# A two-layer hybrid decoder trunk on one core: weights of the third expert block loaded earlier, full blocks first, experts chosen tile by tile, part of the causal mask moved

## The reference

```python
a = rmsnorm(h, mix_norm_g[i]); z = a @ w_in[i]        # split for three mixers
y_a = sgu_mixer(...)                                   # gated unit, mixes tokens in chunks of 128
y_b = conv_mixer(...)                                  # causal convolution, 31 taps, 256 channels
y_c = mla_mixer(...)                                   # 8 heads, causal attention, q and k of 96, v of 64
h = h + concat(rmsnorm(y_a), rmsnorm(y_b), rmsnorm(y_c)) @ w_o[i]
m = rmsnorm(h, ffn_norm_g[i])
h = h + hier_moe(m, ...)                               # 32 experts in 4 groups, 2 experts per token
gate = sigmoid(rmsnorm(h) @ ple_gate_w[i])
h = h + gate * rmsnorm(p[i] @ ple_proj_w[i])           # per-layer embeddings p, "projected"
```

## Time and profile before

| what | value |
|---|---|
| median of 3 runs | 2188.45 us (2186.95 to 2190.23) |
| the profiled execution | 2190.58 us, span 2188.80 us |
| TensorE busy | 2000.5 us, 91% of the span |
| VectorE busy | 1009.4 us, 46% |
| ScalarE busy | 638.8 us, 29% |
| transfers | 361.98 MB, mean 165 GB/s |

### The profile page before, as it was taken

One profiled execution on the slowest core, in us unless ns is written; L12 is line 12 of the kernel. 1 busy time (PEld: TensorE's weight loads), 2 busy tenths in 40 slices (PEclk: granted clock), 3 DMA queues, 4 the chain that ended last, 5 costly groups with the idle time before them and its releaser, 6 DMA issues.

```text
span 2188.8 us, 34749 instructions
## 1 busy us (share of the span) xinstructions
PE 2000.5 (91%) x9032; PEld 1110.8 (51%) x9032; DVE 1009.4 (46%) x2247; ACT 638.8 (29%) x1521; POOL 374.5 (17%) x542
## 2 busy tenths in 40 slices
PE   6999799899969999989979998998999699999898
PEld 3555466655535455544435554666555354445344
DVE  2489756654341111124434897566543421111253
ACT  3333355522111111131133333555221111111221
POOL 2232100021012222210022221000210122221100
PEclk9999899999979999999989998999999799999999
DMA  7011241000389999955210112410004799999422
GB/s 249 15 29 29 59 153 30 25 20 29 140 308 396 380 382 378 389 217 192 88 29 15 29 29 61 152 30 25 20 29 154 292 393 381 377 380 353 175 87 96
DMA packets 122222, 361.98 MB, mean 165 GB/s; under 512 B 18853, under 2 KB 54005, under 8 KB 105220
## 3 DMA queue, kind: packets, MB, share of 16 engines
q1 hardware_dynamic: 105028, 318.74, 40.2%
q0 software_dynamic: 14784, 33.59, 4.1%
q10 hardware_dynamic: 2304, 8.39, 0.9%
HBM read 319.50 MB, written 59.51 MB: 173 GB/s over the span
## 4 chain that ended last, share of the span: by engine, by line
PE 76%; DMA 11%; DVE 5%; issue 4%; ACT 3%; SPq 1%; DVEq 0%; POOL 0%; ACTq 0%; POOLq 0%
PE ps L1801 30%; DMA region_c<-in_moe_w_up_dram 8%; PE ps L2160 7%; PE ps L1964 5%; PE ps L1822 4%; PE ps L2156 4%; PE ps L1996 3%; PE ps L2181 3%; PE ps L1976 3%; PE ps L1770 3%; PE ps L2175 2%; PE ps L2141 2%; PE ps L1896 2%; DMA region_a<-in_moe_w_up_dram 2%; PE ps L2082 2%
## 5 line engine op out<-in xcount | busy, mean ns | idle before, releaser
L1801 PE MATMUL ps<-region_b,region_c 128*128 128x512 f32 x1024 | 451.5, 597 | 7.7 <-DVE region_c L1269 7.7
L1801 PEld LDWEIGHTS ps<-region_b,region_c 128*128 128x128 f32 x1024 | 192.8, 191 | 234.4 <-issue 233.9
L1801 PE MATMUL ps<-region_a,region_c 128*128 128x512 f32 x512 | 225.3, 594 | 0.0
L1680 DVE SCALAR_TENSOR_TENSOR region_a<-region_a,ps 128x128 f32<-128x128 f32 x66 | 23.4, 354 | 387.0 <-ACT region_a L1132 382.7
L2160 PE MATMUL ps<-region_c,region_a 128*128 128x512 f32 x336 | 148.8, 596 | 12.9 <-DMA region_c<-in_moe_w_up_dram 12.8
L1801 PEld LDWEIGHTS ps<-region_a,region_c 128*128 128x128 f32 x512 | 96.9, 191 | 118.0 <-issue 118.0
L1460 DVE TENSOR_REDUCE neg_max<-ps 128x1 f32<-128x128 f32 (+7 forms) x128 | 97.0, 758 | 109.8 <-PE ps L1967 109.0
L1964 PE MATMUL ps<-region_c 96*128 96x512 f32 (+3 forms) x384 | 146.9, 492 | 0.0
L1132 ACT ACTIVATE region_a<-ps 128x128 f32<-128x128 f32 x66 | 21.8, 330 | 364.7 <-PE ps L2160 243.5
L1976 PE MATMUL ps<-ident,region_a 128*128 128x128 f32 x576 | 91.1, 285 | 25.2 <-ACT region_a L1064 25.0
L2160 PEld LDWEIGHTS ps<-region_c,region_a 128*128 128x128 f32 x336 | 62.1, 190 | 92.9 <-issue 92.9
(11 more groups left out here) (351 smaller groups left out, 3065.4 us busy)
## 6 DMA issues: line engine op xcount, KB each, us to landing
region_c<-in_moe_w_gate_dram SPq DMA_DIRECT2D x44, 1024.0 KB
region_c<-in_moe_w_up_dram SPq DMA_DIRECT2D x44, 1024.0 KB
region_c<-in_moe_w_down_dram SPq DMA_DIRECT2D x44, 1024.0 KB
region_a<-in_moe_w_gate_dram SPq DMA_DIRECT2D x22, 1024.0 KB
region_a<-in_moe_w_up_dram SPq DMA_DIRECT2D x22, 1024.0 KB
region_a<-in_moe_w_down_dram SPq DMA_DIRECT2D x22, 1024.0 KB
region_c<-choice_outputs SPq DMA_DIRECT2D x32, 512.0 KB, 4.4
qk_heads<-gains SPq DMA_DIRECT2D x32, 384.0 KB, 3.9
```

The lines of the kernel that those rows point to most:

```text
L1801: ins = mm(dst, lhsT[:, k, :], w[:, k, a:b], start=(k == 0), stop=(k == KD - 1))
```

## The change

- SyncE loads the third block's gate and up once projection 3 is done on TensorE, and waits for the stored embeddings only before its down matrix.
- Pairs are laid out full block first, half block second; all `small` flags swap. If the last half place is empty, it is not done (`no_last`). The counts of half and full blocks done are kept apart.
- Experts are chosen tile by tile: a stage `choose` with 15 instructions, on up to 32 columns, stands behind `g_main` in the output product's loop. The 23 wide ones go. The exponentials of the group gaps move behind "e_diff", "g_sum" and "g_w" behind the comparisons.
- "owner_f" and "owner_i" (now two instructions) stand right behind "key".
- In attention the mask of tiles 3 to 7 is added by VectorE in PSUM before the maximum; TensorE's mask product stays for tiles 0 to 2.

```diff
+    MASKED = 3
...
@@ block loop (step(b, here, nxt, last, small, i)) @@
-                             u % 2 == 0, 3 * i + u // 2)
+                             u % 2 == 1, 3 * i + u // 2)
@@ SyncE @@
-                for b in range(3):
-                    if b == 2:
-
-                        for u in range(2):
-                            sp.wait_ge(e_stored[u], 16 * PAIRS * l + 8 * EARLY_P + 16)
-                        settle(sp, passed)
+                for b in range(2):
                     load_dn(load_gu(b, b), b)
-                prev, n, half = counters(sp, l, passed, halves=True)
+                sp.wait_ge(*P_pe.before(TILES * l + EARLY_P))
+                settle(sp, passed)
+                third = load_gu(2, 2)
+                for u in range(2):
+                    sp.wait_ge(e_stored[u], 16 * PAIRS * l + 8 * EARLY_P + 16)
+                settle(sp, passed)
+                load_dn(third, 2)
+                prev, n, done = counters(sp, l, passed, halves=True)
...
@@ GpSimd @@
                 for u in range(3):
-                    rows = HALF if u % 2 == 0 else P
+                    rows = HALF if u % 2 == 1 else P
...
-                gather(3, 0, prev + 3, False)
+                gather(3, 0, prev + 3, True)
@@ ScalarE @@
-                act.wait_ge(*K_vec.after(l, "g_diff"))
-                nc.scalar.activation(rs(1, TILES, NG), rs(0, TILES, NG), ACT.Exp).then_inc(*K_act.next("g_exp"))
...
                 act.wait_ge(*K_vec.after(l, "e_diff"))
+                nc.scalar.activation(at(A, 7824, TILES, NG), at(A, 7680, TILES, NG), ACT.Exp).then_inc(*K_act.next("g_exp"))
...
-                x_lo(prev, True)
-                tanh(prev, True)
-                x_lo(prev + 1, False)
-                h_evac(prev, True)
+                x_lo(prev, False)
+                tanh(prev, False)
+                x_lo(prev + 1, True)
+                h_evac(prev, False)
@@ VectorE @@
                 def row_max(hh, j):
                     v.wait_ge(*S_pe.after(hh, f"s{j}"))
+                    if j >= MASKED:
+                        own = banks(2 * (j % 2))[:, j * P:(j + 1) * P]
+                        v.tensor_tensor(own, own, mask_b[:, :], ALU.add).then_inc(*X_mask.next(f"mask{j}"))
+                        v.wait_ge(*X_mask.after(hh, f"mask{j}"))
...
+                def choose(t, u, i):
+                    g = TILES * l + t
+
+                    def link(ins, name):
+                        ins.then_inc(*CH_vec.next(name))
+                        v.wait_ge(*CH_vec.after(g, name))
+
+                    v.wait_ge(*G_vec.after(g))
+                    g_max, g_first, m1, i1, m2, i2 = (span(sm(k), t, 1) for k in (0, 3, 4, 5, 6, 7))
+                    gl_, el = lg[:, t, 0:NG], lg[:, t, NG:NG + NE]
+                    link(v.tensor_reduce(g_max, gl_, AX.X, ALU.max), "g_max")
+                    link(v.tensor_scalar(g_gap[:, t, :], gl_, g_max, None, ALU.subtract), "g_diff")
+                    link(v.scalar_tensor_tensor(g_cand, gl_, g_max, order[:, 0:NG], ALU.is_lt, ALU.add), "g_cand")
+                    link(v.tensor_reduce(g_first, g_cand, AX.X, ALU.min), "g_first")
+                    link(v.tensor_scalar(g_far, order[:, 0:NG], g_first, -BIG, ALU.not_equal, ALU.mult), "g_far")
+                    link(v.tensor_tensor(e_in.rearrange("p (g e) -> p g e", g=NG), el.rearrange("p (g e) -> p g e", g=NG),
+                                         g_far.unsqueeze(2).to_broadcast([P, NG, EPG]), ALU.add), "e_in")
+
+                    def largest(src, top, where, hot, n):
+                        link(v.tensor_reduce(top, src, AX.X, ALU.max), f"m{n}")
+                        link(v.scalar_tensor_tensor(cand, src, top, order[:, :], ALU.is_lt, ALU.add), f"cand{n}")
+                        link(v.tensor_reduce(where, cand, AX.X, ALU.min), f"i{n}")
+                        v.tensor_scalar(hot, order[:, :], where, None, ALU.is_equal).then_inc(*CH_vec.next(f"hot{n}"))
+
+                    largest(e_in, m1, i1, hot1[:, t, :], 1)
+                    v.wait_ge(*CH_vec.after(g, "hot1"))
+                    link(v.scalar_tensor_tensor(e_rest, hot1[:, t, :], -2 * BIG, e_in, ALU.mult, ALU.add), "rest")
+                    largest(e_rest, m2, i2, hot2[:, t, :], 2)
+
...
-                             (3, late(conv_scale)), (3, late(conv_silu)), (0, w_main(1)), (-1, g_main), (3, late(conv_out))])
+                             (3, late(conv_scale)), (3, late(conv_silu)), (0, w_main(1)), (-1, g_main), (-1, choose), (3, late(conv_out))])
...
-                link(v.tensor_reduce(sm(0), gl_, AX.X, ALU.max), "g_max")
...
-                link(v.tensor_tensor(picked_b, hot1, hot2, ALU.add), "picked")
+                v.wait_ge(*CH_vec.before(TILES * l + TILES))
+                v.tensor_tensor(picked_b, hot1, hot2, ALU.add).then_inc(*K_vec.next("picked"))
...
                 link(v.scalar_tensor_tensor(keys[:, 3], keys[:, 2], 512.0, keys[:, 1], ALU.mult, ALU.add), "key")
+                owner = rs(9, TILES, NE).rearrange("p a b -> p (a b)")[0:1, 64:64 + POS].bitcast(I32)
+                v.wait_ge(*K_pe.after(l, "owners"))
+                link(v.tensor_copy(owner, ps[0:1, 6, 256:256 + POS]), "owner_f")
+                at_place = cells[0:1, 0:POS].rearrange("p (r a) -> p a r", a=2)
+                link(v.tensor_scalar(at_place[:, 0], owner[:, NE:POS], NE - 1, None, ALU.bitwise_and), "owner_full")
+                link(v.tensor_scalar(at_place[:, 1], owner[:, 0:NE], NE - 1, None, ALU.bitwise_and), "owner_i")
...
-                link(v.tensor_scalar(total, n_pairs[0:1], 2.0, None, ALU.mult), "n_blocks")
+                no_last = last_rows[0:1, 208:209]
+                link(v.tensor_scalar(no_last, n_half[0:1], n_pairs[0:1], 1.0, ALU.is_ge, ALU.subtract), "no_last")
+                link(v.scalar_tensor_tensor(total, n_pairs[0:1], 2.0, no_last, ALU.mult, ALU.add), "n_blocks")
...
+                v.wait_ge(*K_act.after(l, "g_exp"))
+                link(v.tensor_reduce(sm(1), at(A, 7824, TILES, NG), AX.X, ALU.add), "g_sum")
+                link(v.reciprocal(sm(2), sm(1)), "g_w")
...
+                link(v.tensor_copy(cells[0:1, POS + 7:POS + 8], run[:, 5:6]), "smalls")
                 link(v.tensor_tensor(run[:, 0:1], run[:, 0:1], total, ALU.add), "run_n")
+                link(v.tensor_tensor(run[:, 4:5], run[:, 4:5], n_pairs[0:1], ALU.add), "run_pairs")
+                small_now = last_rows[0:1, 210:211]
+                link(v.tensor_tensor(small_now, no_last, n_pairs[0:1], ALU.add), "small_now")
+                link(v.tensor_tensor(run[:, 5:6], run[:, 5:6], small_now, ALU.add), "run_small")
...
-                v.tensor_scalar(by_kind(idx), kinds, 3 * SEQ - 1, None, ALU.bitwise_and).then_inc(*K_vec.next("list_i"))
+                v.tensor_scalar(by_kind(idx)[:, 0], kinds[:, 1], 3 * SEQ - 1, None, ALU.bitwise_and).then_inc(*K_vec.next("list_full"))
+                v.tensor_scalar(by_kind(idx)[:, 1], kinds[:, 0], 3 * SEQ - 1, None, ALU.bitwise_and).then_inc(*K_vec.next("list_i"))
@@ TensorE, scores @@
-                        mm(bank(b + c // 512, 0, w), q, k_ring[u][0:QK, c:c + w], start=True, stop=not last, skip_group_check=True)
+                        ins = mm(bank(b + c // 512, 0, w), q, k_ring[u][0:QK, c:c + w], start=True, stop=not last or j >= MASKED,
+                                 skip_group_check=True)
+                    if j >= MASKED:
+                        ins.then_inc(*S_pe.next(f"s{j}"))
+                        return
 
                     d = (j * P) % 512
                     mm(bank(b + j // 4, d, d + P), ident_b[:, :], mask_b[:, :], start=False, stop=True,
```

More of the change, by code:

```diff
@@ L359, in build @@
         S_pe, O_pe = steps("s_pe", [f"s{j}" for j in tiles]), steps("o_pe", [f"o{m}" for m in couples])
+        X_mask = steps("x_mask", [f"mask{j}" for j in tiles if j >= MASKED])
         B_pe = steps("b_pe", [f"back{m}" for m in couples])
@@ L677, in _ @@
                 for u in range(2):
-                    sp.wait_ge(y_stored[u], (half + pairs) * 16)
+                    sp.wait_ge(y_stored[u], (done[u] + (pairs if u else smalls)) * 16)
                 settle(sp, passed)
@@ L1119, in _ @@
                     embedded(t)
[L1122 removed]
+                prev, n, done = counters(act, l, passed, halves=True)
                 def x_lo(m, small):
```

106 lines of the change are left out of this document (40 added, 66 removed).

## The result

The changed kernel takes 2214.45 us (median of 4 runs, 2210.24 to 2217.18), the kernel before 2189.34 (4 runs): ratio 1.0111, 95% interval 1.0094 to 1.0128, so 21 to 28 us slower. The profiled execution took 2210.24 us, span 2208.50, the fastest of its four; against the profile of before it is 19.7 us longer.

What follows compares the result with a forecast made beforehand. Transfer engines bound the expert stage, with TensorE nearly full; TensorE partly bounds attention. Attention -5.0, loop +0.4, layer 0 -0.6 and layer 1 +2.8 sum to -2.4 us: median 2186.0, own range 2181 to 2191, 2177 to 2195 with unknown bounds.

Steps and rivals of the forecast that it cites:

- attention: Attention, both layers: moving 5 of 8 masks to VectorE saves TensorE time, -5.0 us (outer ends -12 and +2).
- first weight load, from the output product's start: Before the expert stage: first load 1.3 us earlier per layer, with the output product's loop +0.2 us per layer.
- idle stream: Expert stage: transfer engines idle 5 us, then 3 us; less 1.3 us of early start, +6.5 us a layer (3 to 9).
- empty block less skipped steps: Layer 0's expert stage: dropping the empty half block gives -8.3 us, skipped loop steps cost +1.2 us.
- end of layer 1's stage: End of layer 1's expert stage: last block is now a half one, -3.7 us (0 to -3.7).
- Choice by tile: Output product's loop: 3.3 us a tile, mostly hidden, +0.2 us per layer; last normalization 2.1 us late; early choice gains 0.
- Early owners: Routing chain: owner cells written right behind the last key end at 609.8 instead of 613.3, -3.5 us.
- Lists and first product: Expert stage's start: lists 3.8 us later, gather +0.8, transposes and copies +0.6, full product +3.4; first product ends 8.6 us later.
- rival B: Expert stage: full first product at low clock throughout, 14 us instead of 7, slot 0 later, +7.5 us, 2193.5; chance 0.20.
- rival C: Attention: VectorE's mask additions don't hide, +27 us and no gain, about 2215 us; chance 0.06.
- A: Attention: masks worth 0.15 us everywhere, 12 us, giving 2179 us; chance 0.26 with its like.
- Third block's weights: Expert stage: issued earlier they only join the full transfer queue, 0 us; nothing added for the gather.

Runs made afterwards that it cites:

- b_full: Kernel before with only full block first, half block second, and no empty last block: 2197.88 us, ratio 1.0035.
- a_wide: Changed kernel with the choice of experts again as wide instructions behind the output product's loop: 2196.77 us, ratio 1.0035.
- a_last: Changed kernel with only tile 6's choice moved behind the last normalization, done together with tile 7's: 2207.52 us, ratio 1.0087.
- a_behind: Changed kernel with each tile's choice moved behind `conv_out` in the output product's loop: 2208.74 us, ratio 1.0087.
- b_owners: Kernel before with only "owner_f" and "owner_i" moved right behind "key": 2186.28 us, ratio 0.9984.
- b_ot: Kernel before with early owners and the third block's gate and up loaded behind projection 3: 2186.14 us, ratio 0.9984.
- b_ow8: Kernel before with early owners and 8 added 512-column products while TensorE waits for the first gather: 2183.88 us, ratio 0.9974.
- a_warm: Changed kernel with the wide choice behind the loop and 14 added 512-column products while TensorE waits for the first gather: 2190.76 us, ratio 1.0002.

## Why the prediction was wrong

The prediction was a balance of terms, and with two of them mis-sized (the choice in the loop, and the first full product with the idle stream behind it) it tipped. The experiments add up to the whole: full blocks first costs 7.6 us alone (b_full), the choice in the loop 17.7 (a_wide), together 25.3 of the 25.1 us measured, and masks, early owners and the third block's weights brought nothing visible on top of the full-first order: a_wide, which has them all, and b_full, which has none of them, have the same ratio of 1.0035 (medians +6.5 and +7.6 us). Against the profiled executions, both layers together:

| term | predicted | measured |
|---|---|---|
| attention | -5.0 | -3.1 |
| first weight load, from the output product's start | -2.4 | +11.5 |
| idle stream | +16 | +21.7 |
| empty block less skipped steps | -7.1 | -7.1 (worked out, borne out by b_full) |
| end of layer 1's stage | -3.7 | -1.7, or nothing (below) |
| left over | | +2.2 |

(The predicted column adds up to -2.2 us instead of -2.4 by rounding.) The measured ones, with -1.7 for the end, give +23.5 us; the -3.8 us of stretches that the change doesn't touch (-1.6, -1.7 and -0.5 in the table above) bring it to the 19.7 of the profile, and the medians differ by 25. The second row holds the loop, and so the 1.7 us by which the loop's first product of layer 0 was shorter by chance.

**Choice by tile: the step that failed.** Two numbers of it were wrong, its price and the wait that it causes. The price of a tile was worked out as 15 x 0.22 us from the routing chain, whose addresses are constants; in the loop it is 15 x 0.31 = 4.6 us. And of its place only the last normalization and the slack of 1.3 us at c_silu were weighed, as if the choice moved c_silu by a part of its length. It stands ahead of `conv_out`, which starts a chain through ScalarE, GpSimd, normalization and transposes that fills the step; so c_silu came some 2.2 us later against TensorE's own progress (the slack of 1.3 and a wait of 0.93). "+2.1" became +3.9, the longer wait for the last normalization, and "+0.2" became the rest of the loop's loss: 8.5 - 3.9 = 4.6 us in layer 0, 9.8 - 3.9 = 5.9 in layer 1, and some 5.9 in both like for like (a_last, a_behind, a_wide). That "picked" early gains nothing was right: rank products 9.30 us after projection 0, before 9.28. The rule of the Trainium skill, "VectorE: DVE Perf Modes", section on the TRN2 errata, that many small tiles pay the fixed cost each time, pointed the right way; the trace adds that the cost was not the same in both places.

**Early owners** gave the 3.5 us named, in the load (3.6 and 3.2 us). In the changed kernel the gain vanishes in the idle stretch; alone it is worth some 4 us in all (b_owners). The prediction set it down as a gain in full.

**Lists and first product.** The first gather started 1.6 and 2.0 us later after projection 0 (1.7 predicted), and took 9.74 and 9.11 us, +1.9 and +0.7 (0.8). The product was longer by 4.6 and 3.7 us, not 3.4, since most of it ran at the low clock: 9.71 and 10.05 us. So rival B came to hold in part, at the very 10 us from which it was to decide. Its price didn't follow from its own numbers: 14 us against the forecast's 5.1 + 3.4 = 8.5 us are 5.5 us more, not 3 to 4.

**Idle stream:** the mechanism was right, its size was not: 9.9 and 11.8 us instead of 8, since the first product came and ended later than forecast (lines above), and the low clock in front of it was priced only as the half product had shown it. In layer 1 the second product ran at the low clock too, 5.36 instead of 3.67 us.

**End of layer 1:** the half block's shorter product was counted as gain, but behind it TensorE's sequencer still had the skipped steps before it. From the start of the last gate and up product the end is 19.0 us before and 17.4 after, which gives the -1.7. From the issue of the last down matrix it is not shorter: 2042.88 - 2015.51 = 27.4 us before, 2063.09 - 2034.50 = 28.6 after. Which of the two counts is not shown.

**Masks:** -1.5 and -1.7 us in place of -2.5; the additions hid, so rival C fell, and A too. That C's 2215 us is nearly the measured time is chance: none of its 27 us came. 48 products at 0.06 us are 2.9 us, the lower end that was given. **Third block's weights:** nothing in the medians, as said, but "I add nothing" for the gather was not borne out by the profile of b_ot.

What stays open: 1.8 us of layer 1's stage, which is about what the end's -1.7 us would leave if they were nothing; why the changed kernel's other runs are 3 to 7 us above its profiled one (their granted clock is 0.961 to 0.963 against 0.965, no more is recorded); and the true worth of the masks, 0.7 us alone by the medians, 5.2 us on top of early owners and added products.

## What to carry over

Before work is moved into a loop, price its instructions by rows of that loop and not by rows of written-out code, and look at what is queued behind it on its engine: every chain that leaves the engine there can be late by up to its full length. When a stage is bound by transfers, the first thing to ask of a change is when the first buffer comes free; an earlier first load is worth only as much as the first reload follows it. And a saving that ends in front of another engine's queue (here the rank products behind two projections) is none.

## What the runs showed of the hardware

- The same 15 chained VectorE instructions, on up to 32 columns, took 4.6 us in a hardware loop and 3.7 us in written-out code. One pair of them followed at 0.34 and at 0.22 us (570.75 and 600.91 above), with equal durations of 0.19 and 0.24 us; another at 0.22 to 0.23 us in both. Why is not shown.
- TensorE's granted clock was 0.50 (1.2 GHz) in the windows of its wait for the first gather, and the first full product behind it took 9.71 and 10.05 us instead of 7.03. With 8 products in that wait the half product behind them took 3.67 us, the pace of the full clock, in both layers (b_ow8; 5.12 and 6.38 us before). The Trainium skill, "TensorE: Matmul & The Clock Gate", Part 1, says that an idle array gets half the clock and that activity releases it; these runs agree.
- Yet in layer 0 of a_warm the full product took 8.80 us behind 14 us of added products, at a granted clock of 0.81, and in layer 1 7.11 us. Why the clock fell there again is not shown.
